# Gate broadcasts and one-column products of the even layer issued between the halves and tiles of the input projection

## Chip, cores and metric

One core of a Trainium2 chip. The number is the device time of one execution in microseconds; runs before the change: 1102.5, 1107.6 and 1111.56 us, median 1107.6 us.

## What is computed

One inference step of a two-layer decoder for a prompt of 256 positions and 8 sample positions (264 columns together). The change lies in the mixer of the even layer (layer 0):

```python
z = h @ P['ev_w_in'][e]
qkv, zg, b_raw, a_raw, hq, hf, hi, hg = _split(z, ...)
q, k, v = ...                       # causal conv, silu, l2norm
beta = jax.nn.sigmoid(b_raw)
g = -jnp.exp(A_log) * jax.nn.softplus(a_raw + dt_bias)
o_a, S_gdn_new = gated_delta_rule(q, k, v, beta, g, S_gdn)    # prompt and samples, 8 heads of 64
f = lb + (1.0 - lb) * jax.nn.sigmoid(hf)
o_b, S_hg_new = hgrn2_recurrence(qh, 1.0 - f, jnp.log(f), hi, S_hg)
```

For a sample, which has one position, the output of each head is `S^T q`: a 64x64 state per sample and head times one column. There are 8 samples and 8 heads, so 64 such products for the delta rule and 64 for HGRN2.

## The kernel before

All activations are kept with features on the 128 partitions and the 264 positions on the free axis. Each engine's instructions are written out by hand in program order. `make_plan` lists every result that TensorE (PE) leaves in PSUM in `order`; entry number n uses bank n mod 8, a consumer counts `psum_full` up to n + 1, and PE may reuse a bank when `psum_free` of it was raised. `begin`/`end` take the next entry; `open_`/`close` open one ahead of its turn. Weights come through a ring of four slots, two tiles of an input projection to a slot, loaded by SP; SP takes a slot again when the last tile read from it has closed.

`lin(name, m, ...)` is one tile of a projection: 8 f32 products of 128x128 weights with `h` (264 columns), 16 PE instructions in the trace (each f32 product is two). The stretch of the change, in PE's order:

1. `ev_in_a` tiles 0 to 15 (q, k, v for m < 12, the output gate `zg` for m = 12 to 15); head norms `hn` (one product with `bd`) after tiles 4 to 11. After each of tiles 12 to 15, `gate_rows_out(c)` (c = m - 12) spreads rows of `gs`, which lie on 8 partitions, over 128: `bcB`, `bcG` (264 columns), `bcL` (256) and two products for `gr`; 10 PE instructions with 8 active rows.
2. DVE consumes them for each c: `zg` from PSUM, an l2 norm, then behind `full(dve, ("bcL", c))` the products `vb`, `kb`, `bk`, `qe`, a copy to `egc`, `ke`, and four steps to `dt_` out of `gr`. PE's transposes `trk`, `trv` (L1269) wait until DVE has drained `bcL` of c = 3; then come `KK`, on which DVE waits with `mt`, `X1`, and the doubling steps `T1`, `Z`.
3. `ev_in_b` tiles 0 to 7 between the steps of the delta rule, then `su` (state update of the samples), tiles 8 to 11, `state_out("gdn", ...)`: the 64 one-column products (128 PE instructions, 64 rows by 64 columns of weights, 1 moving column) into bank `sO gdn`. They wait for `sst_ready` 4, raised by DVE's last addition to the sample states.
4. ACT copies `sO gdn` to `oT` (`so_copy`), then takes four exponentials of 1024 columns, then the squares of the `gdn` head norm; PE runs tiles 12 to 15 with `hn gdn` 0 to 3 after them, each waiting for a square (`hsq_ready`).
5. POOL loads the HGRN2 states (`shs`) when `sO gdn` is full. PE waits for `hq_ready` and `shs_in`, then issues the 64 products of `sO hgrn` and one with `bd`; after that transposes `htk`, `htv`, the prompt's `att` (masked on DVE, L2332), `kv` (8 steps of a chain on DVE), and `ho`, which waits for the chain's third step; then the projection `ev_out`.

Of the kernel before, what the change touches and what calls it, by code (L numbers as in the profile page):

```python
# [26 lines left out]
L = 256  # L27
NS = 8
T = L + NS
H = 8  # L30
HC = 4
# [92 lines left out]
def make_plan():  # L124
    order, slots, slot_of = [], [], {}
    used = [0]

    def lin(name, tiles, per_slot, cols, first=0, after=None):
        for m in range(first, tiles):
            if m % per_slot == 0:  # L130
                slots.append(("w", name, m // per_slot, cols, None))
            slot_of[(name, m)] = len(slots) - 1
            order.append(("lin", name, m))
            slots[-1] = slots[-1][:4] + (("lin", name, m),)
            if after:
                after(m)
# [51 lines left out]
    lin("ev_in_a", 12, 2, 2048, 8, lambda m: order.append(("hn", "l2", m - 4)))  # L188
    lin("ev_in_a", 16, 2, 2048, 12, lambda m: order.extend([(n, m - 12) for n in ("bcB", "bcG", "bcL", "gr")]))
    for t in range(NCH):  # L190
# [108 lines left out]
def build(nc, A):  # L299
# [17 lines left out]
    with ExitStack() as ctx:  # L317
# [14 lines left out]
        def bank(key):  # L332
            return banks[no[key] % NBANK]
# [917 lines left out]
        def _(pe):  # L1251
# [158 lines left out]

            def state_out(name, st, q, n):
                pe.wait_ge(sst_ready, 4 * n)
                b = begin(("sO", name))
                for c in range(HC):
                    for s in range(NS):
                        for p in range(2):
                            ps = slice(64 * p, 64 * p + 64)
                            ins = mm(b[ps, c * NS + s:c * NS + s + 1], st[ps, c, s, :], q[ps, c, L + s:L + s + 1])
                end(ins)

# [15 lines left out]

            def gate_rows_out(c):

                if c == 0:
                    pe.wait_ge(gate_rows, 5)  # L1440
                    pe.wait_ge(gate_written, 1)
                    pe.wait_ge(con2_in, 16)
                for name, r, w in (("bcB", 0, T), ("bcG", 2, T), ("bcL", 3, L)):
                    b = begin((name, c))
                    end(mm(b[:, 0:w], cst("selc", i=c, p=8), gs[0:8, r, 0:w]))
                b = begin(("gr", c))
                for p in range(2):
                    ins = mm(b[:, p * L:(p + 1) * L], cst("selh", i=2 * c + p, p=8), gs[0:8, 4, 0:L])
                end(ins)

            for m in range(16):
                lin("ev_in_a", m, KC, 2, h, T)
                if 4 <= m < 12:
                    hn("l2", m - 4, T, bd)
                if m == 7:
                    gate_columns()
                if m >= 12:
                    gate_rows_out(m - 12)
            for t in range(NCH):
# [116 lines left out]
            for m in range(8, 12):  # L1576
                lin("ev_in_b", m, KC, 2, h, T)
            state_out("gdn", sgs, qkv, 1)
            for m in range(12, 16):
                lin("ev_in_b", m, KC, 2, h, T)  # L1580
                if m >= 12:
                    hn("gdn", m - 12, T, bd)
            pe.wait_ge(hq_ready, 1)
            pe.wait_ge(shs_in, 16)
            b = begin(("sO", "hgrn"))
            for c in range(HC):
                for s in range(NS):
                    for p in range(2):
                        ps = slice(64 * p, 64 * p + 64)
                        mm(b[ps, c * NS + s:c * NS + s + 1], shs[ps, c, s, :], qfs[ps, c, s:s + 1])  # L1590
            end(mm(b[:, 32:64], bd, qks.rearrange("p c s -> p (c s)")))
            pe.wait_ge(hg_dve, 2)
# [1314 lines left out]
```

## Time and profile before

| | us |
|---|---|
| runs, median (lowest to highest) | 1107.6 (1102.5 to 1111.56) |
| profiled execution, span from first to last instruction | 1106.6 |
| mean granted TensorE clock | 0.953 |
| PE busy | 1037.4 (94%) |
| DVE busy | 656.0 (59%) |
| ACT busy | 385.3 (35%) |

For the profiled execution the span is the only time given. The page's slices, the chain of waits, the instructions in order of time and the busy time of chosen stretches are the views used. A start is counted from the span's start; "[1.31 <-DVE ...]" is idle time of the engine before the row and what ended it; in a table of stretches the columns are start:end, length, busy time and count of PE, weight loads, DVE, ACT and POOL, then granted clock (1.00 is 2.4 GHz, 0.50 is 1.2 GHz), DMA share and GB/s. The busy time of a row of merged instructions runs to the modelled end of its last one, so that the start of the next row tells better when PE went on.

### The profile page before, as it was taken

What the parts mean: (1) busy time and instruction counts of PE and PEld (TensorE: products, weight loads), DVE (VectorE), ACT (ScalarE), POOL (GpSimd) and SP (SyncE); (2) the same over time, 40 slices, a digit from 0 to 9 for tenths busy, and PEclk for the clock granted to TensorE, in tenths of its full rate; (3) what the DMA queues carried; (4) which work ended last, traced back from release to release, by engine and by line L of the source; (5) the groups of instructions that cost most, each with busy time, mean ns of one, the idle gap of its engine ahead of it and who ended that gap; (6) DMA issues with size and microseconds to landing.
All of it is one profiled execution on the core that took longest, in us unless ns stands there. A gap on an engine that the chain in (4) does not pass through costs nothing.

```text
span 1106.6 us, 20808 instructions
## 1 busy us (share of the span) xinstructions
PE 1037.4 (94%) x8340; PEld 901.6 (81%) x8340; DVE 656.0 (59%) x1419; ACT 385.3 (35%) x720; POOL 101.6 (9%) x202
## 2 busy tenths in 40 slices
PE   7998999999998999999999788688999899999996
PEld 5877988877885999999987555367788689999996
DVE  6865716135333789986656466377241368998652
ACT  3533222523144444444412112432223454444430
POOL 0010001230000012211000000001000001211100
PEclk9988999869998999999999887889999999999999
DMA  8421124413744454564554967764834535555530
GB/s 332 147 89 40 42 82 152 152 45 114 283 167 197 160 186 166 182 233 165 180 178 146 353 222 235 242 212 177 320 139 161 219 121 170 178 188 204 187 150 40
DMA packets 41569, 192.44 MB, mean 174 GB/s; under 512 B 4602, under 2 KB 5754, under 8 KB 24578
## 3 DMA queue, kind: packets, MB, share of 16 engines
q1 hardware_dynamic: 36146, 167.39, 43.4%
q0 software_dynamic: 4288, 22.15, 5.2%
q10 hardware_dynamic: 1040, 1.57, 0.4%
q8 instruction: 66, 1.08, 0.4%
q14 instruction: 29, 0.24, 0.1%
HBM read 183.74 MB, written 7.35 MB: 173 GB/s over the span
## 4 chain that ended last, share of the span: by engine, by line
PE 74%; issue 9%; DVE 5%; SPq 5%; DMA 4%; ACT 2%; POOL 0%; DVEq 0%; ACTq 0%; POOLq 0%
PE bank L1266 73%; SPq L655 3%; SPq L641 2%; DVE work L1945 2%; DMA ring<-in_od_in 2%; DMA ring<-in_ck 1%; DVE work L1948 1%; PE bank L1269 1%; ACT work L811 1%; DMA ring<-in_pool_v 1%; ACT work_r L811 1%; DVE work L2727 1%; DMA x<-in_x 0%; DVE ring_r L1945 0%; DVE sq L1945 0%
## 5 line engine op out<-in xcount | busy, mean ns | idle before, releaser
L1266 PE MATMUL bank<-h,ring 128*128 128x264 f32 x896 | 215.0, 397 | 2.2 <-DMA ring<-in_od_in 2.2
L1266 PEld LDWEIGHTS bank<-h,ring 128*128 128x128 f32 x896 | 174.1, 196 | 36.5 <-issue 5.8
L1266 PE MATMUL bank<-h_r,work_r 128*128 128x264 f32 x704 | 200.6, 285 | 0.0
L1266 PE MATMUL bank<-h_r,ring_r 128*128 128x264 f32 x704 | 200.2, 284 | 0.0
L1266 PE MATMUL bank<-sq_r,work_r 128*128 128x264 f32 x704 | 199.8, 284 | 0.0
L811 ACT ACTIVATE work_r<-ring 128x2048 fp32r<-128x2048 f32 (+1 forms) x60 | 125.0, 2087 | 191.2 <-PE bank L1266 191.2
L1945 DVE TENSOR_TENSOR ring_r<-ring,work_r 128x2048 fp32r<-128x2048 f32 (+1 forms) x60 | 150.2, 2505 | 45.3 <-ACT work_r L811 45.2
L1266 PEld LDWEIGHTS bank<-sq_r,work_r 128*128 128x128 f32 x704 | 132.6, 188 | 0.1
L1266 PE MATMUL bank<-work_r 128*128 128x264 f32 x704 | 129.7, 285 | 3.0 <-DVE ring_r L1945 2.9
L1266 PEld LDWEIGHTS bank<-h_r,ring_r 128*128 128x128 f32 x704 | 132.4, 188 | 0.0
L1266 PEld LDWEIGHTS bank<-h_r,work_r 128*128 128x128 f32 x704 | 132.2, 188 | 0.1
L1266 PE MATMUL bank<-work 64*64 64x64 f32 (+12 forms) x1472 | 116.0, 289 | 15.5 <-DVE work L1945 7.1
L1266 PEld LDWEIGHTS bank<-work 64*64 64x64 f32 (+6 forms) x1472 | 82.8, 159 | 44.8 <-issue 29.1
L811 ACT ACTIVATE work<-bank 128x512 f32<-128x512 f32 (+3 forms) x143 | 55.0, 432 | 169.8 <-PE bank L1266 138.0
L1266 PEld LDWEIGHTS bank<-work_r 128*128 128x128 f32 x704 | 109.0, 188 | 4.0 <-issue 3.9
L1266 PE MATMUL bank<-work_r,ring_r 128*128 128x264 f32 x352 | 100.0, 284 | 0.0
L1266 PE MATMUL bank<-mix,ring 128*128 128x264 f32 x384 | 92.2, 402 | 1.5 <-ACT mix L811 1.5
L1266 PEld LDWEIGHTS bank<-mix,ring 128*128 128x128 f32 x384 | 76.1, 199 | 16.0 <-issue 2.2
L1948 DVE SCALAR_TENSOR_TENSOR work<-work,vec 128x256 f32<-128x256 f32 x224 | 84.1, 412 | 4.4
L1266 PE MATMUL bank<-work,ring 128*128 128x256 f32 (+2 forms) x432 | 81.6, 360 | 0.0
L1266 PEld LDWEIGHTS bank<-work,ring 128*128 128x128 f32 (+1 forms) x432 | 68.4, 173 | 9.9 <-issue 0.5
L1945 DVE TENSOR_TENSOR work<-work 128x512 f32<-128x512 f32 (+8 forms) x94 | 59.5, 671 | 21.6 <-ACT work L811 20.1
(256 smaller groups left out, 1092.7 us busy)
## 6 DMA issues: line engine op xcount, KB each, us to landing
ring<-in_gu SPq DMA_DIRECT2D x44, 1024.0 KB, 4.9
ring<-in_down SPq DMA_DIRECT2D x16, 1408.0 KB, 6.0
ring<-in_pool_k SPq DMA_DIRECT2D x64, 256.0 KB, 3.6
ring<-in_pool_v SPq DMA_DIRECT2D x64, 256.0 KB, 3.2
ring<-in_ev_in_a SPq DMA_DIRECT2D x8, 1024.0 KB, 6.7
ring<-in_ev_in_b SPq DMA_DIRECT2D x8, 1024.0 KB, 4.8
work<-in_cv POOLq DMA_DIRECT2D x8, 1024.0 KB, 12.7
ring<-in_ck SPq DMA_DIRECT2D x8, 1024.0 KB, 4.9
```

The source lines that it names most:

```text
L641: numbers = [sp.value_load(pages[0:1, at:at + 1], min_val=0, max_val=POOL_PAGES - 1) for s_ in (s0_, s0_ + 1) for at in (PAGES * s_ + 2 * ...
L655: sp.dma_start(dst[:, 512 * j:512 * (j + 1)].unsqueeze(1), pool[bass.ds(page, 1)].rearrange("a p n -> p a n")).then_inc(ring_full[s % SLOT ...
L811: return nc.scalar.activation(out, in_, func, **k)
L1266: return nc.tensor.matmul(out, lhsT, rhs, start=start, stop=stop, skip_group_check=True)
L1269: return nc.tensor.transpose(out, in_, ident)
L1945: return V.tensor_tensor(out, a, b, op)
L1948: return V.scalar_tensor_tensor(out, a, s, b, op0, op1)
L2727: V.tensor_tensor_scan(gg[:, b, m, q, :], mag2[:, n:n + 1].broadcast_to([128, LS]), ta[:, b, m, q, :], 0.0, ALU.mult, ALU.add).then_inc(s5 ...
```

## The change

Tiles 13 to 15 of `ev_in_a` are issued in two halves of four products each (`half_product`, which was there already for other projections). Between the halves stand `bcB` and `bcG` of c = m - 13 (`gate_factors`), behind the second half `bcL` and `gr` of it; the four broadcasts of c = 3 come together at the end. The 64 products of `sO gdn` go out in four parts of 16 behind tiles 8, 9, 10 and 11 of `ev_in_b`, the wait for `sst_ready` standing before the first. The 64 of `sO hgrn` go out behind the head norms of tiles 13, 14 and 15, the last two parts together; the waits for `hq_ready` and `shs_in` move to the first part. `order` is changed to match for the broadcasts; for the one-column products it stays, since their bank is opened ahead. No instruction is added or taken away.

PE, tiles 12 and 13 of `ev_in_a` with the broadcasts of c = 0; `work,con` are `gs` and the selecting constants. Before:

```order
L1266 MATMUL bank<-h,ring 128x264 [waits ring_full2,psum_free7]
L1266 MATMUL bank<-h,ring 128x264 x7
L1266 MATMUL bank<-work,con 128x264 [waits con2_in,psum_free0,gate_written,gate_rows]
L1266 MATMUL bank<-work,con 128x264 [waits psum_free1]
L1266 MATMUL bank<-work,con 128x256 [waits psum_free2]
L1266 MATMUL bank<-work,con 128x256 [waits psum_free3]
L1266 MATMUL bank<-work,con 128x256
L1266 MATMUL bank<-h,ring 128x264 [waits psum_free4]
L1266 MATMUL bank<-h,ring 128x264 x7
```

and now:

```order
L1271 MATMUL bank<-h,ring 128x264 [waits ring_full2,psum_free7]
L1271 MATMUL bank<-h,ring 128x264 x7
L1271 MATMUL bank<-h,ring 128x264 [waits ring_full2,psum_free2]
L1271 MATMUL bank<-h,ring 128x264 x3
L1271 MATMUL bank<-work,con 128x264 [waits con2_in,psum_free0,gate_written,gate_rows]
L1271 MATMUL bank<-work,con 128x264 [waits psum_free1]
L1271 MATMUL bank<-h,ring 128x264 [waits ring_full2]
L1271 MATMUL bank<-h,ring 128x264 x3
L1271 MATMUL bank<-work,con 128x256 [waits psum_free3]
L1271 MATMUL bank<-work,con 128x256 [waits psum_free4]
L1271 MATMUL bank<-work,con 128x256
```

Tile 13 is split, the broadcasts of c = 0 moved from before it to its middle and its end, and the banks by which they wait are others.

PE, tiles 8 and 9 of `ev_in_b` (`h,ring`) and the products of `sO gdn` (`64x1`); a row "x63" or "x15" is the rest of a burst. Before, with tile 12 and the first `hn gdn` behind it:

```order
L1266 MATMUL bank<-h,ring 128x264 [waits ring_full0,psum_free1]
L1266 MATMUL bank<-h,ring 128x264 x7
L1266 MATMUL bank<-h,ring 128x264 [waits psum_free2]
L1266 MATMUL bank<-h,ring 128x264 x7
L1266 MATMUL bank<-work 64x1 [waits psum_free5,sst_ready]
L1266 MATMUL bank<-work 64x1 x63
L1266 MATMUL bank<-h,ring 128x264 [waits ring_full2,psum_free6]
L1266 MATMUL bank<-h,ring 128x264 x7
L1266 MATMUL bank<-hsq,con 128x264 [waits hsq_ready,psum_free7]
```

and now tiles 8 to 10:

```order
L1271 MATMUL bank<-h,ring 128x264 [waits ring_full0,psum_free1]
L1271 MATMUL bank<-h,ring 128x264 x7
L1271 MATMUL bank<-work 64x1 [waits psum_free5,sst_ready]
L1271 MATMUL bank<-work 64x1 x15
L1271 MATMUL bank<-h,ring 128x264 [waits psum_free2]
L1271 MATMUL bank<-h,ring 128x264 x7
L1271 MATMUL bank<-work 64x1 x16
L1271 MATMUL bank<-h,ring 128x264 [waits ring_full1,psum_free3]
L1271 MATMUL bank<-h,ring 128x264 x7
L1271 MATMUL bank<-work 64x1 x16
```

The wait for `sst_ready` stands three tiles earlier, and each part of 16 products has a tile of 8 before and behind it.

PE, tiles 14 and 15 of `ev_in_b` and the products of `sO hgrn`, up to the first transpose (`con,work 128x128`). Before:

```order
L1266 MATMUL bank<-h,ring 128x264 [waits ring_full3,psum_free2]
L1266 MATMUL bank<-h,ring 128x264 x7
L1266 MATMUL bank<-hsq,con 128x264 [waits hsq_ready,psum_free3]
L1266 MATMUL bank<-h,ring 128x264 [waits psum_free4]
L1266 MATMUL bank<-h,ring 128x264 x7
L1266 MATMUL bank<-hsq,con 128x264 [waits hsq_ready,psum_free5]
L1266 MATMUL bank<-work 64x1 [waits psum_free6,shs_in,hq_ready]
L1266 MATMUL bank<-work 64x1 x63
L1266 MATMUL bank<-work,con 128x32
L1269 MATMUL bank<-con,work 128x128 [waits psum_free7,hg_pool,hg_dve]
```

and now:

```order
L1271 MATMUL bank<-work 64x1 [waits psum_free6,shs_in,hq_ready]
L1271 MATMUL bank<-work 64x1 x15
L1271 MATMUL bank<-h,ring 128x264 [waits ring_full3,psum_free2]
L1271 MATMUL bank<-h,ring 128x264 x7
L1271 MATMUL bank<-hsq,con 128x264 [waits hsq_ready,psum_free3]
L1271 MATMUL bank<-work 64x1 x16
L1271 MATMUL bank<-h,ring 128x264 [waits psum_free4]
L1271 MATMUL bank<-h,ring 128x264 x7
L1271 MATMUL bank<-hsq,con 128x264 [waits hsq_ready,psum_free5]
L1271 MATMUL bank<-work 64x1 x32
L1271 MATMUL bank<-work,con 128x32
L1274 MATMUL bank<-con,work 128x128 [waits psum_free7,hg_pool,hg_dve]
```

Of 64 products 32 stand together ahead of the transposes, where there were 64; the wait for the loaded states stands before tile 14. The rows of DVE, POOL and SP are the same in both, and ACT's differ only in the bank that three of them wait for.

```diff
--- before.py
+++ after.py
@@ -125,8 +125,10 @@
     order, slots, slot_of = [], [], {}
     used = [0]
 
-    def lin(name, tiles, per_slot, cols, first=0, after=None):
+    def lin(name, tiles, per_slot, cols, first=0, after=None, before=None):
         for m in range(first, tiles):
+            if before:
+                before(m)
             if m % per_slot == 0:
                 slots.append(("w", name, m // per_slot, cols, None))
             slot_of[(name, m)] = len(slots) - 1
@@ -186,7 +188,10 @@
     lin("ev_in_a", 8, 2, 2048, 4, lambda m: order.append(("hn", "l2", m - 4)))
     order.append(("gc",))
     lin("ev_in_a", 12, 2, 2048, 8, lambda m: order.append(("hn", "l2", m - 4)))
-    lin("ev_in_a", 16, 2, 2048, 12, lambda m: order.extend([(n, m - 12) for n in ("bcB", "bcG", "bcL", "gr")]))
+    lin("ev_in_a", 13, 2, 2048, 12)
+    lin("ev_in_a", 16, 2, 2048, 13, lambda m: order.extend([("bcL", m - 13), ("gr", m - 13)]),
+        lambda m: order.extend([("bcB", m - 13), ("bcG", m - 13)]))
+    order.extend([(n, HC - 1) for n in ("bcB", "bcG", "bcL", "gr")])
     for t in range(NCH):
         order.extend([("trk", t), ("trv", t)])
     G4 = [(t, par) for t in range(NCH) for par in range(2)]
@@ -1408,15 +1413,14 @@
                     b = begin(("su", name, c))
                     end(mm(b[:, :], bd, w2[:, c, :, :].rearrange("p s v -> p (s v)")))
 
-            def state_out(name, st, q, n):
-                pe.wait_ge(sst_ready, 4 * n)
-                b = begin(("sO", name))
-                for c in range(HC):
-                    for s in range(NS):
-                        for p in range(2):
-                            ps = slice(64 * p, 64 * p + 64)
-                            ins = mm(b[ps, c * NS + s:c * NS + s + 1], st[ps, c, s, :], q[ps, c, L + s:L + s + 1])
-                end(ins)
+            def state_out(name, c, st, q, first):
+
+                b = open_(("sO", name)) if c == 0 else bank(("sO", name))
+                for s in range(NS):
+                    for p in range(2):
+                        ps = slice(64 * p, 64 * p + 64)
+                        ins = mm(b[ps, c * NS + s:c * NS + s + 1], st[ps, c, s, :], q[ps, c, first + s:first + s + 1])
+                return ins
 
             b = begin(("ab",))
             pe.wait_ge(vec_in, 16)
@@ -1434,28 +1438,38 @@
                     ins = mm(b[:, t * H:(t + 1) * H], gs[0:8, 4, t * 128:(t + 1) * 128], ident[0:8, 0:H])
                 end(ins)
 
-            def gate_rows_out(c):
+            def gate_factors(c):
 
                 if c == 0:
                     pe.wait_ge(gate_rows, 5)
                     pe.wait_ge(gate_written, 1)
                     pe.wait_ge(con2_in, 16)
-                for name, r, w in (("bcB", 0, T), ("bcG", 2, T), ("bcL", 3, L)):
-                    b = begin((name, c))
-                    end(mm(b[:, 0:w], cst("selc", i=c, p=8), gs[0:8, r, 0:w]))
+                for name, r in (("bcB", 0), ("bcG", 2)):
+                    b = open_((name, c))
+                    close(mm(b[:, 0:T], cst("selc", i=c, p=8), gs[0:8, r, 0:T]), (name, c))
+
+            def gate_rows_out(c):
+
+                b = begin(("bcL", c))
+                end(mm(b[:, 0:L], cst("selc", i=c, p=8), gs[0:8, 3, 0:L]))
                 b = begin(("gr", c))
                 for p in range(2):
                     ins = mm(b[:, p * L:(p + 1) * L], cst("selh", i=2 * c + p, p=8), gs[0:8, 4, 0:L])
                 end(ins)
 
-            for m in range(16):
+            for m in range(13):
                 lin("ev_in_a", m, KC, 2, h, T)
                 if 4 <= m < 12:
                     hn("l2", m - 4, T, bd)
                 if m == 7:
                     gate_columns()
-                if m >= 12:
-                    gate_rows_out(m - 12)
+            for m in range(13, 16):
+                half_product("ev_in_a", m, 0, h)
+                gate_factors(m - 13)
+                half_product("ev_in_a", m, 4, h)
+                gate_rows_out(m - 13)
+            gate_factors(HC - 1)
+            gate_rows_out(HC - 1)
             for t in range(NCH):
                 drained(pe, ("bcL", HC - 1))
                 transposes(("trk", t), [ke[:, c, t * 128:(t + 1) * 128] for c in range(HC)])
@@ -1575,20 +1589,20 @@
             state_update("gdn", ws2, 2)
             for m in range(8, 12):
                 lin("ev_in_b", m, KC, 2, h, T)
-            state_out("gdn", sgs, qkv, 1)
+                if m == 8:
+                    pe.wait_ge(sst_ready, 4)
+                ins = state_out("gdn", m - 8, sgs, qkv, L)
+            close(ins, ("sO", "gdn"))
             for m in range(12, 16):
                 lin("ev_in_b", m, KC, 2, h, T)
-                if m >= 12:
-                    hn("gdn", m - 12, T, bd)
-            pe.wait_ge(hq_ready, 1)
-            pe.wait_ge(shs_in, 16)
-            b = begin(("sO", "hgrn"))
-            for c in range(HC):
-                for s in range(NS):
-                    for p in range(2):
-                        ps = slice(64 * p, 64 * p + 64)
-                        mm(b[ps, c * NS + s:c * NS + s + 1], shs[ps, c, s, :], qfs[ps, c, s:s + 1])
-            end(mm(b[:, 32:64], bd, qks.rearrange("p c s -> p (c s)")))
+                hn("gdn", m - 12, T, bd)
+                if m == 13:
+                    pe.wait_ge(hq_ready, 1)
+                    pe.wait_ge(shs_in, 16)
+                if m >= 13:
+                    state_out("hgrn", m - 13, shs, qfs, 0)
+            state_out("hgrn", HC - 1, shs, qfs, 0)
+            close(mm(bank(("sO", "hgrn"))[:, 32:64], bd, qks.rearrange("p c s -> p (c s)")), ("sO", "hgrn"))
             pe.wait_ge(hg_dve, 2)
             pe.wait_ge(hg_pool, 3)
             for t in range(NCH):
```

## Rows read from the trace of the kernel before

**Rows 1.** The page: span, and the granted clock in 40 slices

```profile
span 1106.6 us, 20808 instructions
...
PEclk9988999869998999999999887889999999999999
```

**Rows 2.** Chain of waits that ended last: start us, us, what

```profile
12.44 74.57 PE bank L1266 x314
...
158.53 63.64 PE bank L1266 x514
```

**Rows 3.** PE in order of time, `ev_in_a` 12 to 15: start us, us, what, [idle]

```profile
63.63 2.45 PE L1266 MATMUL bank<-work,con 8*128 8x264 f32 x10
66.01 5.52 PE L1266 MATMUL bank<-h,ring 128*128 128x264 f32 x16
...
85.41 2.45 PE L1266 MATMUL bank<-work,con 8*128 8x264 f32 x10
89.17 1.97 PE L1269 MATMUL bank<-con,work 128*128 128x128 f32 x16 [1.31 <-DVE work L1945]
```

**Rows 4.** Stretches around `ev_in_a`: length, busy of PE to POOL, clock, DMA

```profile
66.01:71.46 5.45, 5.45 (x18) 4.09 (x17) 2.32 (x9) 1.51 (x3) 0.00 (x0) 0.69 0.00 0
81.66:85.41 3.75, 3.75 (x17) 2.95 (x16) 2.32 (x9) 0.00 (x0) 0.00 (x0) 1.00 0.01 2
89.17:91.06 1.89, 1.89 (x16) 1.72 (x16) 1.52 (x9) 0.89 (x1) 0.00 (x0) 1.00 0.22 82
```

**Rows 5.** DVE in order of time, the first gate stage and the first `KK`

```profile
65.35 1.57 DVE L1945 TENSOR_TENSOR work<-work,bank 128x264 f32<-128x264 f32 x4 [0.38 <-PE bank L1266]
...
66.92 0.41 DVE L1945 TENSOR_TENSOR work<-work,bank 128x256 f32<-128x256 f32 x1
67.24 1.12 DVE L1948 SCALAR_TENSOR_TENSOR work<-bank,gcol,con 128x128 f32<-128x128 f32 x4
...
92.36 1.29 DVE L1948 SCALAR_TENSOR_TENSOR work<-bank,work 64x256 f32<-64x256 f32 x3 [1.60 <-PE bank L1266]
```

**Rows 6.** PE in order of time, `ev_in_b` 8 to `ho`

```profile
179.71 14.40 PE L1266 MATMUL bank<-h,ring 128*128 128x264 f32 x64
...
194.05 4.76 PE L1266 MATMUL bank<-work 64*64 64x1 f32 x128
...
198.73 6.22 PE L1266 MATMUL bank<-h,ring 128*128 128x264 f32 x16
...
217.34 4.26 PE L1266 MATMUL bank<-work 64*64 64x1 f32 x128
...
232.62 11.04 PE L1266 MATMUL bank<-work 128*64 128x128 f32 x144 [1.42 <-DVE work L1945]
```

**Rows 7.** Stretches of the one-column products, transposes, `ho` and `ev_out`; columns of rows 4

```profile
194.00:196.00 2.00, 2.00 (x68) 1.96 (x68) 0.00 (x0) 0.39 (x1) 0.00 (x0) 1.00 0.51 70
221.98:225.57 3.59, 3.59 (x18) 3.26 (x18) 0.81 (x4) 1.79 (x3) 3.08 (x2) 0.50 0.38 79
232.62:234.30 1.68, 1.68 (x34) 1.26 (x34) 1.46 (x4) 0.00 (x0) 0.00 (x0) 1.00 0.04 10
234.40:243.58 9.18, 9.18 (x112) 6.82 (x112) 2.66 (x7) 1.19 (x2) 0.00 (x0) 0.50 0.01 3
243.58:247.26 3.68, 3.68 (x10) 2.86 (x9) 0.00 (x0) 1.92 (x4) 3.49 (x1) 0.50 0.00 0
```

**Rows 8.** DVE and ACT in order of time, beside and behind the one-column products

```profile
180.52 2.49 DVE L1945 TENSOR_TENSOR work<-work 128x512 f32<-128x512 f32 x4
...
198.94 4.03 ACT L811 ACTIVATE work<-work 128x1024 f32<-128x1024 f32 x4
...
202.88 0.41 ACT L811 ACTIVATE hsq<-oT 128x264 f32<-128x264 f32 x1
...
227.74 2.55 DVE L2332 COPY_PREDICATED work<-con,bank 128x512 f32<-128x512 int32 x4 [4.88 <-PE bank L1266]
```

**Rows 9.** DMA issues 50 to 260 us: KB each, us to landing

```profile
work<-in_shs POOLq DMA_DIRECT2D x1, 1024.0 KB, 5.4
```

## Prediction

> **What bounds the kernel now.** I read four views in this order. The page [rows 1] first: the span is 1106.6 us, and the slices of the granted clock are below 9 at the places where PE does something other than wide matmuls. Then the chain of waits [rows 2]: it runs on PE from 12.44 for 74.57 us, and again from 158.53 for 63.64 us, so nearly all of the changed stretch is bound by PE's own stream and what shortens that stream shortens the kernel. Then PE in order of time [rows 3, 6] beside the clock in the same stretches [rows 4, 7]. Last DVE and ACT beside it [rows 5, 8], for what is late next.
>
> What is to be seen: behind the burst of broadcasts at 63.63 a tile of 16 passes starts at 66.01 and the next burst only at 71.46, 5.45 us at a mean clock of 0.69; behind a later burst the same tile takes 3.75 us at clock 1.00 [rows 3, 4]. So the clock fell from 2.4 to 1.2 GHz although PE had been issuing without a pause; what it had issued were products of 8 active rows. Of the four bursts two were followed so (the tile at 73.83 reads like the one at 66.01). The same shows behind the 128 one-column passes of `sO gdn`: 2.00 us hold 68 of them at full clock, the burst takes 4.68 us in all (194.05 to 198.73), and the tile behind it 6.1 us [rows 6, 7] where four tiles in a row take 14.34, that is 3.585 each [rows 6]. Behind `sO hgrn` the 16 transposes take 3.59 us at clock 0.50, those of `trk`/`trv` 1.89 at 1.00 [rows 4, 7]. The change puts full tiles between such passes.
>
> **Part one, the gate broadcasts.** What an interruption costs comes first, as the change makes more of them. A tile with a burst on both sides takes 3.75 us at full clock against 3.585 plain: 0.17. A burst takes 2.38 (63.63 to 66.01) for ten passes, 2.24 at the plain pace of 0.224: 0.14. Together 0.31 us a burst. There were four bursts and there will be six (mid and end of each of three tiles, c = 3 joined to the last): +0.6 us on PE. Against this stand the two slow tiles, 2 x (5.45 - 3.75) = 3.4 us, if no stretch between the bursts lowers the clock any more; each burst is now 0.9 to 1.3 us with 1.8 us of half a tile on either side. I take that it doesn't, up to the last one.
>
> But DVE comes later, because `bcL` of c = 0 now stands behind tile 13 instead of before it. Tile 12 ends at 63.55. One c takes PE a tile and ten broadcasts with two interruptions: 3.585 + 2.2 + 0.6 = 6.4 us. The second half of tile 15 ends at 63.55 + 2 x 6.4 + (1.79 + 0.31 + 0.9 + 1.79) = 81.1. DVE starts a c stage 1.72 us after its burst's start, of which four passes (0.9) are no longer ahead: `vb` of c = 2 at about 82.2. A stage lasts 3.01 (65.35 to 67.24 + 1.12 = 68.36), then `zg` of c = 3 some 0.35, and `ke` of c = 3 ends 1.98 after its `vb` (65.35 to 66.92 + 0.41) [rows 5]: 82.2 + 3.0 + 0.35 + 2.0 = 87.6. The transposes that wait for it start at 87.7 instead of 89.17 [rows 3]: 1.5 us, not 2.8. PE's idle time there grows from 1.31 to some 2.7, since its broadcasts end near 85.
>
> Worse, from 81.1 to 87.7 PE has nothing but broadcasts and waiting; before, that was 85.41 to 89.17 and the transposes still ran at 1.00 [rows 4]. I expect the clock to be low when the transposes start: 3.6 instead of 1.9 us. DVE had waited for the first `KK` until 92.36, 1.30 behind `KK`'s start at 91.06. Now 87.7 + 3.6 + 1.30 = 92.6 with the clock back by then; with it still low, by the 2.17 us between `att`'s start at 225.57 and DVE's at 227.74 [rows 7, 8], 93.5; with no fall at all 90.9. Part one is bounded by -1.5 and +1.1 us; I take +0.2, the value with the clock back, which `att`'s own rows make likely (it was low for 3.59 us of transposes and part of `att`).
>
> **Part two, `sO gdn`.** 32 passes at 2.00 / 68 = 0.029 us are 0.94 us, with the interruption of 0.31 (the broadcasts are the nearest rows; between nothing and 0.4) 1.25 a part. Tile 8 ends at 179.71 + 3.585 = 183.3; the last addition behind `sst_ready` ends at 180.52 + 2.49 = 183.01 [rows 8], so the moved wait costs nothing; if that cover goes, tiles 9 to 11 are queued behind it and each us late is a us lost. Four tiles and four parts end at 179.71 + 14.34 + 5.0 = 199.05, against 198.73: the clock kept and three more interruptions cancel. Tile 12 then takes 3.6 instead of 6.1 us and ends near 202.6. But `hn gdn` 0 waits for ACT: `so_copy` comes when it came, four exponentials end at 198.94 + 4.03, the square at 202.88 + 0.41 = 203.29 [rows 8]. The norm goes out at 203.4 instead of 204.8: 1.4 us won, and 0.8 waited for ACT.
>
> **Part three, `sO hgrn`.** From 203.4: norm 0.45, tile 13 3.6, norm 0.45, a part 1.25, tile 14 and norm 4.0, a part 1.25, tile 15 and norm 4.0, two parts together 1.25 + 0.94, the product with `bd` 0.45: 221.0 against 221.98, so 1.0 us ahead (0.4 lost to two more interruptions). The states, issued at 199.40 and 5.4 us on the way [rows 9], are there at 204.8, before PE asks for them at 207.9. ACT's square roots end 1 us later than before, still ahead of `att`. With the clock kept the transposes take 1.9 instead of 3.6: 2.7 ahead at `att`. Its first result comes 1.30 instead of 2.17 behind its start: 3.6 us ahead at DVE's masking, the start of the chain `att`, `kv`, `ho` that PE waits for (1.42 idle before `ho`) [rows 6, 8]. So `ho` starts 3.6 us earlier.
>
> `ho` itself ran 9.18 us at 0.50, behind 1.68 us at 1.00 [rows 7]. The wait ahead of it shrinks to about 0.7 but its passes stay as narrow, and I leave its clock as it was.
>
> A rule speaks against part of this price. The Trainium skill, "TensorE: Matmul & The Clock Gate", section "Step-by-step: what each phase is for", lets PE pull a weight load ahead of running matmuls, so that an interruption would be free. By it the seven more would cost nothing and the sum would be some 2 us better. The rows show 0.31 us each, so the trace doesn't agree here.
>
> **Sum.** +0.2 - 3.6 = -3.4 us. Against the profiled execution that is 1106.6 - 3.4 = 1103.2; its span is all the page gives of its time, 1.0 us under the median of the runs. On the median: 1104.2 us. Loads and stores are not moved past each other, and SP's loads follow PE's tiles, so later stages keep what is won.
>
> **Rivals.**
> - `ho` keeps the clock too. For: the wait before it is halved, and it began at 1.00. Against: 9.18 us at 0.50 without a return. At the first pace (34 passes in 1.68) its 112 passes take 5.5, so 3.6 us; the product behind it, 3.68 us at 0.50, gives 1.6 more. 1104.2 - 5.2 = 1099.0.
> - Interruptions are free (the loads are pulled ahead). For: none of the rows in question shows a single column at full clock between two tiles. Against: the 0.31 above. 1104.2 - 7 x 0.31 = 1102.0.
> - Slower: the clock falls in the thinned stretches too. The place is tiles 9 to 15 of `ev_in_b`, where now six parts stand with a tile behind each; the price is that of the gate tile, 5.45 - 3.75 = 1.70 each. From the third fall on it decides: two eat the 3.4. With four, 1104.2 + 6.8 = 1111.0. For: the clock fell behind bursts that were shorter than the whole of `sO gdn`. Against: a full tile behind the last gate bursts kept it. [...]
> - The change doesn't do what it says on the path: another wait, DVE's gate stage above all, takes all that PE wins. 1107.6.
>
> **How the numbers follow.** Forecast 0.50 (own range 1100.5 to 1107.5), `ho` at full clock 0.25, free interruptions 0.05, falls in the thinned stretch 0.12, nothing won 0.08. The runs before lie 9 us apart, so one per cent, 11 us, is about what a measurement of this kernel can tell from no change. Faster by over 1% (under 1096.5) needs `ho` and more: a third of its case and a little of the forecast's, 0.12. Slower by over 1% (over 1118.7) needs all six falls and a loss at the gates: 0.04. Within: 0.84. The range takes in `ho`'s case down to 1095.5 and four falls with 1110.5 short of their mean.
>
> **What would show it.** Right: tiles 13 to 15 near 3.9 us without a granted clock under 1; `trk` near 87.7 with over 2 us of idle before it and its transposes at 0.50; the burst rows of `sO gdn` four times near 0.94; `hn gdn` 0 waiting about 0.8 for ACT; `htk` at 1.00. Wrong: transposes of `trk` at 1.00 (1.7 better), any tile of `ev_in_b` 9 to 15 over 4 us, `ho` at 1.00, or a wait of PE for `shs` or `sst_ready`.

## The result, and the profile after

The change made the kernel slower by a little. In the comparison the changed kernel took 1108.99 us (median of 20 runs, 1102.83 to 1115.22) and the kernel before 1105.05 us (20 runs, 1098.6 to 1111.56), a ratio of 1.004, with a 95% interval of 1.0024 to 1.0057. The forecast was 3.4 us faster than before; by the ratio it is some 4.4 us slower. The ratios are not quotients of the medians: they and their intervals leave out three executions that took over 1.5% longer than the fastest of their kernel (2045.3 us in part one alone, 1715.74 with the late multiplication, 1326.63 in the kernel before beside them), while the medians count them.

The page of the changed kernel, to be held against [rows 1]:

```profile
span 1110.6 us, 20810 instructions
...
PEclk9997999959998999999999997879999999999998
```

Of 27.8 us each, the third slice (the gate tiles) and the eighth (194 to 222 us) rose from 8 to 9, the fourth fell from 8 to 7 and the ninth (222 to 250) from 6 to 5. So in the stretch of the one-column products the clock is where the change puts it, up to about 222 us, and something goes wrong behind that. The chain of waits (start us, us, what) names it:

```profile
158.64 40.30 PE bank L1271 x312
200.14 2.95 ACT work L816 x3
203.55 14.71 PE bank L1271 x118
218.76 1.23 issue
221.71 4.50 DVE mix L1959
227.55 37.39 PE bank L1271 x360
```

In [rows 2] PE had the chain from 158.53 for 63.64 us. Now one product of DVE stands in it with 4.50 us, and PE goes on only at 227.55.

PE in order of time around the gates (start us, us, what, idle before it), against [rows 3]:

```profile
66.03 1.15 PE L1271 MATMUL bank<-work,con 8*128 8x264 f32 x4
67.11 2.05 PE L1271 MATMUL bank<-h,ring 128*128 128x264 f32 x8
...
82.14 3.74 PE L1271 MATMUL bank<-work,con 8*128 8x256 f32 x16
88.26 3.68 PE L1274 MATMUL bank<-con,work 128*128 128x128 f32 x16 [2.38 <-DVE work L1959]
```

and from `ev_in_b` tile 8 on, against [rows 6]:

```profile
179.82 3.72 PE L1271 MATMUL bank<-h,ring 128*128 128x264 f32 x16
183.48 1.09 PE L1271 MATMUL bank<-work 64*64 64x1 f32 x32
184.50 3.83 PE L1271 MATMUL bank<-h,ring 128*128 128x264 f32 x16
...
198.85 3.83 PE L1271 MATMUL bank<-h,ring 128*128 128x264 f32 x16
203.55 0.68 PE L1271 MATMUL bank<-hsq,con 128*128 128x264 f32 x2 [0.87 <-ACT hsq L816]
...
220.83 1.95 PE L1274 MATMUL bank<-con,work 128*128 128x128 f32 x16
222.70 1.16 PE L1271 MATMUL bank<-work 64*128 64x128 f32 x16
227.55 18.69 PE L1271 MATMUL bank<-work 64*128 64x128 f32 x288 [3.68 <-DVE oT L1959]
246.17 3.89 PE L1271 MATMUL bank<-mix,ring 128*128 128x264 f32 x8
```

Up to 222.70 this is what was forecast, with `att` 2.87 us ahead of the 225.57 of [rows 7]. Then PE stops after 16 of `att`'s passes and waits 3.68 us. The stretches (columns of [rows 4]) show the clock on either side of this wait: tile 12, the transposes, and then all of `att`'s rest, `kv` and `ho`:

```profile
198.85:202.50 3.65, 3.65 (x20) 2.96 (x16) 1.27 (x2) 3.50 (x5) 2.35 (x2) 1.00 0.99 321
220.83:222.70 1.87, 1.87 (x18) 1.71 (x17) 1.48 (x2) 1.83 (x6) 1.39 (x2) 1.00 0.84 355
227.55:246.17 18.62, 18.62 (x289) 15.12 (x289) 8.65 (x19) 1.18 (x2) 0.00 (x0) 0.50 0.01 3
```

DVE in the same place, against [rows 8]:

```profile
221.19 0.49 DVE L1962 SCALAR_TENSOR_TENSOR tmp<-oT,vec,hr 128x264 f32<-128x264 f32 x1 [3.01 <-ACT hr L816]
221.71 4.50 DVE L1959 TENSOR_TENSOR mix<-tmp,work 128x264 f32<-128x264 f32 x1
226.13 0.48 DVE L1962 SCALAR_TENSOR_TENSOR tmp<-oT,vec,hr 128x264 f32<-128x264 f32 x1
...
227.21 0.19 DVE L1959 TENSOR_TENSOR oT<-work,bank 128x32 f32<-128x32 f32 x1
227.32 1.33 DVE L2346 COPY_PREDICATED work<-con,bank 128x512 f32<-128x512 int32 x2
229.63 1.33 DVE L2346 COPY_PREDICATED work<-con,bank 128x512 f32<-128x512 int32 x2 [0.98 <-PE bank L1271]
230.86 0.40 DVE L2360 COPY work<-bank 128x256 f32<-128x256 f32 x1
```

The third of the four head-norm products `mix` takes 4.50 us; the first takes 0.44 at 216.87. Everything that DVE does behind it is late: the row at 227.21, which drains `sO hgrn`, and the masking. The drain matters more than it looks, since `sO hgrn` is entry n of PSUM's order and the second half of `att` holds entry n + 8, the same bank; so PE's 3.68 us of waiting end with this row. What else ran at 221.71 is on GpSimd (POOL):

```profile
221.29 0.96 POOL L724 DMA_DIRECT2D h<-in_memx  x1 [12.87 <-PE bank L1271]
222.28 3.63 POOL L725 TENSOR_TENSOR work<-work 128x2048 f32<-128x2048 f32 x1
```

The second row multiplies the HGRN2 sample states by their decay. It waits for `full(pool, ("sO", "hgrn"))`, as the issue of the load before it does, and neither line was touched by the change. In the kernel before it stood elsewhere:

```profile
223.46 3.63 POOL L720 TENSOR_TENSOR work<-work 128x2048 f32<-128x2048 f32 x1
```

There the second pair of DVE's head-norm steps and products ran ahead of it:

```profile
220.71 0.49 DVE L1948 SCALAR_TENSOR_TENSOR tmp<-oT,vec,hr 128x264 f32<-128x264 f32 x1 [2.59 <-ACT hr L811]
...
222.10 0.43 DVE L1945 TENSOR_TENSOR mix<-tmp,work 128x264 f32<-128x264 f32 x1
```

DVE's last head-norm product was over at 222.53, and behind the two short steps that drain `sO hgrn` DVE waited 4.88 us for PE until 227.74 [rows 8]: the multiplication lay in a hole of DVE's. The change shrank the hole from both sides. `sO hgrn` is full 1.15 us earlier (its successor, the transposes, 220.83 against 221.98 [rows 7]), and the head norm behind tile 15 goes out later (218.09 against 216.81), with two parts of `sO hgrn` ahead of it where there were none: DVE's first step of the second pair begins at 221.19, where it had begun at 220.71.

### The profile page after: what moved, and what is told of

It is laid out like the page before. It is cut to its first block, busy times and chain, and to the rows that moved or that the text cites. A ratio compares the mean times of both kernels' runs of the same rounds, so it can differ in the third digit from the quotient of the medians.

```text
span 1110.6 us, 20810 instructions
## 1 busy us (share of the span) xinstructions
PE 1035.6 (93%) x8340; PEld 897.5 (81%) x8340; DVE 659.3 (59%) x1419; ACT 385.0 (35%) x720; POOL 101.5 (9%) x202
## 4 chain that ended last, share of the span: by engine, by line
PE 73%; issue 10%; DVE 6%; SPq 5%; DMA 4%; ACT 2%; POOL 0%; DVEq 0%; ACTq 0%; POOLq 0%
PE bank L1271 72%; SPq L660 3%; SPq L646 3%; DVE work L1959 2%; DMA ring<-in_od_in 2%; ACT work L816 1%; DVE work L1962 1%; DMA ring<-in_ck 1%; PE bank L1274 1%; DMA x<-in_x 1%; ACT work_r L816 1%; DVE work L2741 1%; DVE mix L1959 0%; DMA ring<-in_pool_v 0%; DVE ring_r L1959 0%
## 5 line engine op out<-in xcount | busy, mean ns | idle before, releaser
L1271 PE MATMUL bank<-h,ring 128*128 128x264 f32 x896 | 210.2, 390 | 2.0 <-DMA ring<-in_od_in 2.0
L1271 PEld LDWEIGHTS bank<-h,ring 128*128 128x128 f32 x896 | 169.3, 191 | 34.5 <-issue 6.0
L1271 PE MATMUL bank<-work 64*64 64x64 f32 (+12 forms) x1472 | 120.4, 303 | 17.5 <-ACT work L816 5.6
L1271 PEld LDWEIGHTS bank<-work 64*64 64x64 f32 (+6 forms) x1472 | 85.4, 167 | 50.5 <-issue 35.9
```

Of the source, the lines that this page charges most:

```text
L1271: return nc.tensor.matmul(out, lhsT, rhs, start=start, stop=stop, skip_group_check=True)
```

## The experiments

**Theory.** GpSimd's multiplication keeps DVE's product out for as long as it runs, and so delays the drain of `sO hgrn`, the masking, the chain and the clock of `ho`. **Rivals.** The issue of the `h` load on GpSimd, which stands at the same place, is what keeps DVE out; or part one costs the time (its transposes run at 0.50); or parts two and three cost it on PE, by their interruptions.

**The parts alone.** Part one alone, as an edit on the changed kernel; the one-column products stand as before the change:

```diff
-                ins = state_out("gdn", m - 8, sgs, qkv, L)
...
+            state_out("gdn", sgs, qkv, 1)
```

> The kernel before with the gate broadcasts alone between the halves of tiles 13 to 15; the one-column products in one burst each. Theory (GpSimd's multiplication of the sample states holds DVE's product behind the head norm, so the loss lies in the one-column part): transposes trk at about 27.7 us behind the end of tile 12 against 29.2 before, at half clock; time 1104.5 to 1106.5 us, ratio 0.999 to 1.002. Rival G (the loss comes from the gate part): ratio 1.003 to 1.006, some 1109 us. Rival D (the load of memx, not the multiplication, holds DVE): as the theory for this kernel.

Measured: 1105.04 us against 1105.27, ratio 1.0007 (0.9986 to 1.0029). PE in order of time, the transposes behind the gates:

```profile
87.54 3.68 PE L1274 MATMUL bank<-con,work 128*128 128x128 f32 x16 [2.38 <-DVE work L1960]
```

The same wait and the same slow transposes as in the changed kernel, and no time that shows; the interval ends below the 1.003 from which the rival began, so the rival that part one costs it falls.

Parts two and three without part one (the gate lines as before):

> The kernel before with the one-column products in parts alone; the gate broadcasts as before. Theory: the product of DVE into mix behind the third head norm takes 4 to 4.5 us instead of 0.43, PE waits over 3 us ahead of the second half of att, the clock is at half from there through ho; ratio 1.003 to 1.006. Rival G: the loss is gone, ratio 0.995 to 1.000. Rival D: as the theory for this kernel.

Measured: 1108.16 us, ratio 1.0024 (1.0000 to 1.0048), a little under the expected 1.003. The product `mix` took 4.49 us at 219.69, beside a multiplication of 3.63 at 220.25, and PE waited 3.68 for the drain. So the loss sits in these parts. They were then taken one by one. Part two alone:

> The kernel before with only the products of the delta rule in parts; those of HGRN2 in one burst. Theory: hn gdn 0 goes out 1.4 us earlier behind tile 8 than before, and so does everything behind; GpSimd's multiplication again starts behind DVE's products and the burst of HGRN2 lowers the clock as before; no product over 1 us; ratio 0.997 to 1.000. Rival S (parts by themselves cost more than the clock gives): ratio 1.001 to 1.004.

Measured: 1106.25 us, ratio 1.0005 (0.9978 to 1.0031), a little above what was expected, and the expectation of undisturbed products failed. DVE and then GpSimd:

```profile
218.96 4.70 DVE L1942 TENSOR_TENSOR mix<-tmp,work 128x264 f32<-128x264 f32 x1
```

```profile
219.72 3.63 POOL L720 TENSOR_TENSOR work<-work 128x2048 f32<-128x2048 f32 x1
```

With `sO hgrn` in one piece but full earlier, it is the fourth product that is caught; the transposes ran at half clock (3.59 us), so PE itself came late and waited only 1.17 for the drain, and no loss of time shows. Part three alone:

> The kernel before with only the products of HGRN2 in parts; those of the delta rule in one burst. Theory: the last head norm is 2.5 us later against the end of the sample products, GpSimd's multiplication starts before DVE's products of the second pair, one of them takes over 3 us, and PE waits for the drained bank ahead of att; ratio 1.002 to 1.006. Rival S: DVE's products at 0.43 us each, and any loss in the parts' own rows.

Measured: 1110.77 us, ratio 1.0046 (1.0022 to 1.0069). The third product took 4.50 us and PE waited 3.68, as expected. Either part alone moves the two instructions onto each other.

**The multiplication moved away.** The changed kernel with one line more on GpSimd, so that the load's issue stays and the multiplication waits for the chain:

```diff
+            drained(pool, ("kv", 7))
             nc.gpsimd.tensor_tensor(shs, shs, zf[:, :, L:T]...)
```

> The changed kernel with one edit: GpSimd's multiplication of the HGRN2 states of the samples waits until DVE has drained the eighth kv step; the load of memx is issued where it was. Theory: the product into mix is back at 0.43 to 0.5 us, PE waits under 0.5 us ahead of the second half of att, att and kv at clock 1.00, ho starts 5 us or more earlier behind tile 8 of ev_in_b than in the changed kernel (there 47.8 us after tile 9's product burst order, 227.55 for att); ratio to before 0.992 to 0.998, 1096 to 1103 us. Rival D (the load of memx, issued by GpSimd just ahead, or its writes hold DVE): the product still takes over 4 us, PE still waits 3.7, ratio 1.003 to 1.006. Rival G: DVE as in the theory, but the ratio stays above 1.000 by what the gate part costs.

Measured: 1102.56 us, ratio 0.9982 (0.9957 to 1.0006), just above the expected 0.998. DVE:

```profile
221.71 0.43 DVE L1960 TENSOR_TENSOR mix<-tmp,work 128x264 f32<-128x264 f32 x1
...
223.96 2.56 DVE L2347 COPY_PREDICATED work<-con,bank 128x512 f32<-128x512 int32 x4 [0.62 <-PE bank L1272]
226.43 0.39 DVE L2361 COPY work<-bank 128x256 f32<-128x256 f32 x1
```

GpSimd:

```profile
221.28 0.96 POOL L724 DMA_DIRECT2D h<-in_memx  x1 [12.86 <-PE bank L1272]
233.80 3.61 POOL L726 TENSOR_TENSOR work<-work 128x2048 f32<-128x2048 f32 x1 [11.55 <-DVE work L1960]
```

and PE:

```profile
228.84 11.36 PE L1272 MATMUL bank<-work 128*64 128x128 f32 x144 [1.43 <-DVE work L1960]
240.13 2.13 PE L1272 MATMUL bank<-mix,ring 128*128 128x264 f32 x4
```

The same product at the same 221.71, beside the same issue of a load, takes 0.43 us: the rival of the load's issue falls, and so does that of PE's interruptions, which are all still there. The theory holds. By the two ratios the move is worth some 6.4 us (1.0040 against 0.9982).

`ho` starts at 228.84, 3.78 us before the 232.62 of [rows 6], and `ev_out` at 240.13, 6.04 before the changed kernel's. Where these 6.04 lie is seen from the start of `ho` in the changed kernel and from `kv` ahead of it, first there, then here:

```profile
234.06 12.18 PE L1271 MATMUL bank<-work 128*64 128x128 f32 x144
```

```profile
229.56:234.06 4.50, 4.50 (x131) 4.38 (x129) 4.02 (x9) 0.00 (x0) 0.00 (x0) 0.50 0.00 0
```

```profile
224.68:227.42 2.74, 2.74 (x130) 2.60 (x128) 2.60 (x7) 0.00 (x0) 0.00 (x0) 1.00 0.68 245
```

In the changed kernel PE waits for nothing more behind 227.55: it runs the rest of `att`, `kv` and `ho` without a gap at 0.50, so that `ho` follows PE's own work and not DVE's chain. With the late multiplication `kv` runs at 1.00, and PE then waits 1.43 us for the chain. So 5.22 of the 6.04 us lie ahead of `ho` (PE's wait of 3.68 us and the half clock behind it, less that 1.43), and 0.82 in `ho` (11.29 against 12.11), which keeps 1.00 for its first 1.2 us here and never has it there.

The same line in the kernel before:

> The kernel before with the same edit as the one on the changed kernel. All theories: in the kernel before the multiplication ended 0.65 us ahead of DVE's masking, which waited for att, so moving it wins nothing there: ratio 0.999 to 1.002. Should it win as much as on the changed kernel, the multiplication held DVE in both, and the theory that the change brought it onto the path falls.

Measured: 1105.57 us, ratio 0.9995 (0.9972 to 1.0017). Without the collision nothing is won that shows, and a later multiplication does no harm that shows.

The late multiplication with parts two and three only, part one left out:

> The one-column products in parts, without the gate part, and GpSimd's multiplication behind the eighth kv step. Theory: as the changed kernel with the late multiplication (ratio 0.9982) but for the gate part, which was measured at 1.0007: ratio 0.996 to 0.999. If the gate part is worth nothing here too, the two are alike within 0.15%.

Measured: 1101.15 us, ratio 0.9971 (0.9947 to 0.9995). It is the lowest of all ratios, and its interval lies wholly under 1. Against the version with part one (0.9982) the intervals overlap widely: once more part one is worth nothing that shows.

**What kind of exclusion it is.** The changed kernel with the multiplication cut into four quarters, issued back to back (one execution):

```diff
-            nc.gpsimd.tensor_tensor(shs, shs, ..., ALU.mult).then_inc(sdec_ready, 1)
+            for c in range(HC):
+                ins = nc.gpsimd.tensor_tensor(shs[:, c], shs[:, c], ..., ALU.mult)
+            ins.then_inc(sdec_ready, 1)
```

> The changed kernel with GpSimd's multiplication of the HGRN2 sample states cut into four instructions of a quarter each, issued where it was. Theory (DVE's product with two operands in SBUF waits until the GpSimd instruction that runs has ended): the product of the third head norm, 4.50 us in the changed kernel, waits for the end of one quarter at most before DVE gets a turn, so no DVE instruction there takes over 1.5 us, and the second half of att starts under 2 us late instead of 3.7. Rival B (the two engines are slowed by the traffic of both, not by turns): the product still takes about 4 us, since the same bytes pass.

Measured: 1110.2 us. DVE and GpSimd:

```profile
220.45 4.90 DVE L1961 TENSOR_TENSOR mix<-tmp,work 128x264 f32<-128x264 f32 x1
```

```profile
221.01 4.03 POOL L726 TENSOR_TENSOR work<-work 128x512 f32<-128x512 f32 x4
```

This expectation failed, and the sign named for rival B, a product of about 4 us, came. DVE gets no turn between the quarters: its product ends at 225.35, 0.31 us behind the end of the last quarter (225.04). In the changed kernel it is the same 0.30 (226.21 against 225.91), and with part two alone 0.31 (223.66 against 223.35). That both engines are slowed, as rival B has it, is not borne out: GpSimd's whole multiplication takes 3.63 us beside the held product and 3.61 by itself (233.80 above). Why DVE gets no turn between the quarters is not shown. Cutting the instruction doesn't help; moving it does.

The changed kernel with the multiplication behind the drain of `sO hgrn`, beside the masking:

```diff
+            drained(pool, ("sO", "hgrn"))
             nc.gpsimd.tensor_tensor(shs, shs, zf[:, :, L:T]...)
```

> After the change, GpSimd's multiplication of the HGRN2 sample states put behind DVE's drain of `sO hgrn`: it then lies beside DVE's masking of `att` (one operand from PSUM, the mask from SBUF) and the first steps of the `kv` chain. Theory that only DVE instructions with two SBUF operands are kept out: the fourth head-norm product takes 0.43 us as with the late multiplication, the masking takes 0.64 us each and ends near 226.5 although GpSimd works beside it, the first chain product with two SBUF operands (226.9 there) waits at most to the end of the multiplication (begun near 223.2, so 226.8 to 227.2), and `ho` starts within 0.4 us of 228.84: ratio 0.995 to 1.001. Rival, any DVE instruction that touches SBUF is kept out: the masking starts only near 226.9, the chain 3 us later, and `ho` at 231.5 to 232: ratio 1.000 to 1.004.

Measured: 1102.43 us, ratio 0.9980 (0.9953 to 1.0006). DVE, GpSimd and PE:

```profile
226.41 2.57 DVE L2347 COPY_PREDICATED work<-con,bank 128x512 f32<-128x512 int32 x4 [2.25 <-PE bank L1272]
```

```profile
224.25 3.61 POOL L726 TENSOR_TENSOR work<-work 128x2048 f32<-128x2048 f32 x1 [1.18 <-DVE oT L1960]
```

```profile
221.65 3.39 PE L1275 MATMUL bank<-con,work 128*128 128x128 f32 x16
```

GpSimd multiplies until 227.86, and the masking that begins at 226.41 takes its usual 2.57 us for four (2.55 in [rows 8]). Its one operand comes from PSUM, so the rival that any DVE instruction is kept out falls. The start of `ho`, 231.30, missed the expected 228.84: 0.83 us of it was there at tile 8 (180.64 against 179.81), and the transposes ran mostly at half clock in this execution (0.55 from 221.65 to 224.97), which put PE late, not DVE. The first chain product began at 229.38, behind the multiplication, and so tells nothing.

All kernels side by side, from the start of `ev_in_b` tile 8 to the start of `ev_out` in the profiled executions (us), with the longest `mix` product and the ratio to the kernel before:

| kernel | tile 8 to `ev_out` | longest `mix` | ratio |
|---|---|---|---|
| before | 63.87 | 0.43 | 1 |
| changed | 66.35 | 4.50 | 1.0040 |
| part one alone | 61.74 | 0.43 | 1.0007 |
| parts two and three | 66.35 | 4.49 | 1.0024 |
| part two alone | 63.21 | 4.70 | 1.0005 |
| part three alone | 67.60 | 4.50 | 1.0046 |
| changed, multiplication late | 60.32 | 0.43 | 0.9982 |
| parts two and three, late | 61.91 | 0.43 | 0.9971 |
| changed, behind the drain | 62.18 | 0.43 | 0.9980 |
| before, late | 63.98 | 0.43 | 0.9995 |
| changed, four quarters | 66.73 | 4.90 | (one execution) |

The kernels in which the third product was caught (4.49 to 4.90) and PE waited 3.68 us or more are the slow ones. One row warns against reading a single execution too finely: part one alone shows 61.74, 2.1 less than before, in a stretch that it doesn't touch and without a gain in the ratio; there the granted clock merely fell less. Behind the stretch the executions differ too: near 340 us a row of 36 passes took 4.70 us in the three kernels that have parts and a later multiplication, and 6.25 to 6.40 in the other eight. Whether that belongs to the move was not tried; it is why the ratios and not the spans carry the comparison.

## Why the prediction was wrong

The kernel came out slower where a gain of 3.4 us was forecast. The mechanism that was to bring the gain is there; what failed is the step of part three from `att` to "3.6 us ahead at DVE's masking". It took DVE as free when `att`'s first result comes, and put at nothing what DVE does ahead of the masking: the second pair of head-norm steps and products, and the drain of a bank that `att` needs. Nor did it ask what GpSimd starts on the event that the change brings forward (`sO hgrn` full). The sentence before, "ACT's square roots end 1 us later than before, still ahead of `att`", holds as far as it goes (221.46 against 220.98, with `att` at 222.70), but asks only whether ACT is late. In place of the 3.6 us won, the runs showed a DVE product of 4.50 us instead of 0.43, a wait of 3.68 us on PE, and half clock from there through `ho`.

- Part one, on PE: tile 12 started 0.62 us later in this execution (60.60 against 59.98), before anything is changed. Less that, the transposes came at 87.64 (forecast 87.7) after 2.38 us of idle (forecast 2.7) at clock 0.50 for 3.68 us (forecast 3.6). DVE's first masking of `KK` came at 94.09, less the offset 93.47: the case "still low" with 93.5, not the chosen 92.6. So the term was +1.1 at that point, but in part one alone it was given back. In the kernel with part one alone that masking is at 93.37, 1.01 later than before, and the second group of products of the doubling steps starts at 107.77 in both: the clock came back by 104 us in the one and during 104 to 106 in the other (0.65 and 0.50 from 102 to 104). A term of +0.2 fits the ratio of part one alone, 1.0007, but its interval (0.9986 to 1.0029, some -1.5 to +3.2 us) is too wide to show it.
- Part two: right. A part's row takes 1.02 us (183.48 to 184.50) and the tile behind it 3.76 instead of 3.585. Four tiles and parts took 19.03 us (forecast 19.34), which leaves 0.23 for an interruption (estimated 0.31). Tile 12 ran at 1.00, and the first head norm went out at 203.55 after 0.87 us of waiting for ACT (forecast 203.4 and 0.8).
- Part three on PE: right. The transposes started at 220.83 (forecast 221.0), ran 1.87 us at 1.00, and `att` began at 222.70. PE waited neither for the states nor for `sst_ready`.
- Part three on DVE: wrong. The masking was to start 3.6 us earlier, near 224.1. It started at 227.32, with its second half at 229.63, and the chain's first copy came at 230.86, where it had been 230.20 before. With the multiplication out of the way that copy comes at 226.43, 3.77 earlier, and `ho` 3.78 earlier. So the term of -3.6 was of the right size in that execution, although the wait ahead of `ho` did not shrink to 0.7 (1.43). Against it stood an unpriced term: in the changed kernel DVE's first copy is 4.43 us later than with the multiplication out of the way, and `ho` 5.22 us later.
- `ho`: the forecast left its clock as it was, 1.68 us at 1.00 and then 0.50. With the late multiplication that is nearly so (1.2 us at 1.00). In the changed kernel the clock was at 0.50 when PE went on at 227.55, as it was in all four executions with a wait of 3.68 us or more at this place, and it stayed there through `ho`. Against the kernel before this makes the balance: `ho` starts 1.44 us later (234.06 against 232.62; 0.11 of it was there at tile 8) and takes 12.11 us instead of 10.96, together the 2.59 us by which `ev_out` is late (246.17 against 243.58).
- The rivals: "another wait takes all that PE wins" named the right kind of event, but put DVE's gate stage there and let it take the gain at most; it took 6.04 where some 3.5 had been won (243.58 less 240.13). The fall of the clock in the thinned stretches (1111.0 us) came near in time and was refuted: tiles 9 to 15 took 3.56 to 3.76 us each, tile 12 at 1.00. Free interruptions are refuted by the 0.23 above. In the rival of `ho` at full clock, the 1.6 us for the product behind it doesn't come out of the rows, as half of 3.68 is 1.84; nothing rests on it.
- The signs: those listed for "right" came, and none of those listed for "wrong". All of them were PE's; no sign stood for DVE's products or for GpSimd, where the forecast failed.

The trace of before had the mechanism in it, in rows that the prediction doesn't use, 55 us ahead of the place. DVE, and beside it GpSimd:

```profile
165.15 2.29 DVE L1945 TENSOR_TENSOR work<-con,work 128x2048 f32<-128x2048 f32 x1
167.47 5.60 DVE L1945 TENSOR_TENSOR work<-work 128x2048 f32<-128x2048 f32 x1
```

```profile
165.26 5.66 POOL L700 TENSOR_TENSOR work<-work,egc 128x2048 f32<-128x2048 f32 x1 [1.51 <-DVE work L1945]
```

A DVE product of this shape takes 2.29 us or 5.60, and GpSimd's takes 5.66 here and 3.63 at 223.46. Read with what the runs showed, the rows fit two engines that wait for each other in turn: from the end of DVE's first product (167.44) to the end of GpSimd's (170.92) are 3.48 us, near its 3.63, and DVE's second is done 2.15 behind that, at 173.07. No run tests this reading at that place. Together with the multiplication that starts 0.93 us behind DVE's last head-norm product, it would have given a rival on the slow side.

## What to carry to other kernels

When a change brings an event forward, list every engine that waits for it, not only the one on the critical path, and lay what each then starts beside what the others do at that moment. In this kernel the GpSimd instruction of 3.6 us did no harm that shows where it was tied to an event that DVE itself raises (behind the chain, or beside a masking that reads PSUM); where it only happened to lie in a hole of DVE's, the next change of order moved the two onto each other. Where the same operation shows two durations in a trace, read what ran beside the longer one before any forecast.

## What was not expected of the hardware

- A DVE product of 264 columns with both operands in SBUF, 0.43 us long, took 4.49 to 4.90 us beside a GpSimd multiplication of 3.63 to 4.03 us, and ended 0.30 to 0.31 us behind it each time; a DVE masking with one operand in PSUM was not held up. The Trainium skill, "SBUF — State Buffer", section "Who interferes with whom", has a DVE instruction with two SBUF inputs contend with a GpSimd instruction that reads SBUF, and calls contention an exclusive lock. The traces agree in this (0.43 us without GpSimd's multiplication, 4.49 to 4.90 with it). Of the modes in which DVE takes both ports the section says that whoever issues first has them for the whole instruction. If that held here, a series of four short instructions would let DVE in after the first, and it didn't (4.90 us).
- The product that is kept out starts 0.57 us ahead of GpSimd's multiplication in the profile (221.71 and 222.28) and would have been over by then. What holds it before GpSimd's profiled start is open; it isn't the load's issue, beside which the same product took 0.43.
- Under the same order of PE's instructions from tile 8 of `ev_in_b` on, the transposes behind `sO hgrn` ran at 1.00 in some executions (the changed kernel, with and without the late multiplication) and at 0.55 to 0.59 in others (the multiplication behind the drain; parts two and three with the late one). What decides it was not tried.
